# State space batches: input products ahead of the lag products, tiles shared 2, 3, 3, 3, fine rotation table by group

## The reference

```
u, q, k, v, og, glr = split(rms_norm(x) @ w_in)          # 17 column tiles of up to 128
lam_bar = exp(lam * step)                                 # complex, 32 groups x 64 states, two directions
bu = einsum('gpc,blgc->blgp', b_bar, u)                   # 16 channels a group
state_t = lam_bar * state_(t-1) + bu_t                    # forward, and reversed for the other direction
y = real(einsum('gcp,blgp->blgc', c, states)), both directions, + d * u
y = gelu(y); y = y * sigmoid(y @ w_glu)                   # the sigmoid part is in a later stage
```

## Time and profile before

| | us |
|---|---|
| median of 3 runs (2537.19 to 2540.1) | 2537.8 |
| the profiled execution, its own time | 2539.81 |
| its span | 2538.0 |
| PE busy | 2443.0 (96%) |
| DVE busy | 1531.7 (60%) |
| ACT busy | 1150.5 (45%) |
| mean granted TensorE clock | 0.986 |

### The profile page before, as it was taken

The page is one execution under the profiler, slowest core; times in us unless marked ns, Lnnn a source line. Parts: engine busy times, 40 slices in busy tenths (PEclk is TensorE's granted clock), DMA queues, the critical chain, the costliest instruction groups (busy, mean ns, idle before and its releaser), DMA issues.

```text
span 2538.0 us, 35247 instructions
## 1 busy us (share of the span) xinstructions
PE 2443.0 (96%) x14102; PEld 2075.0 (82%) x14102; DVE 1531.7 (60%) x2599; ACT 1150.5 (45%) x2010; POOL 0.2 (0%) x4
## 2 busy tenths in 40 slices
PE   7997799899999999999999999999999999999999
PEld 4887576778888999899778888778788888888887
DVE  8988756767546755564565446656886645533332
ACT  4232336344433555544454444445665443423422
POOL 0000000000000000000000000000000000000000
PEclk9998899999999999999999999999999999999999
DMA  5324532255312455444224323223334423433332
GB/s 189 95 67 103 167 111 96 80 169 191 108 59 85 156 183 184 123 132 136 78 73 157 116 81 119 75 84 101 92 92 142 132 73 88 141 99 100 92 100 91
DMA packets 109667, 289.24 MB, mean 114 GB/s; under 512 B 18913, under 2 KB 41569, under 8 KB 108225
## 3 DMA queue, kind: packets, MB, share of 16 engines
q1 hardware_dynamic: 101392, 261.36, 33.5%
q10 hardware_dynamic: 8112, 25.63, 3.1%
HBM read 265.35 MB, written 19.50 MB: 112 GB/s over the span
## 4 chain that ended last, share of the span: by engine, by line
PE 81%; DVE 12%; ACT 4%; issue 2%; DMA 1%; SPq 0%; ACTq 0%; DVEq 0%
PE ps L1414 65%; PE ps L1504 2%; PE ps L338 2%; PE ps L1479 2%; PE ps L334 2%; DVE wlo L1391 1%; PE ps L1522 1%; PE ps L1546 1%; DVE ps L1697 1%; DVE ps L1696 1%; DVE yP L1698 1%; ACT yP L1565 1%; DMA wraw<-wt 1%; DVE x L555 1%; PE ps L1446 1%
## 5 line engine op out<-in xcount | busy, mean ns | idle before, releaser
L1414 PE MATMUL ps<-in_hP,whi 128*128 128x512 f32 x1336 | 541.1, 405 | 1.6 <-issue 1.6
L1386 ACT ACTIVATE whi<-wraw 128x1024 fp32r<-128x1024 f32 x430 | 452.2, 1053 | 194.1 <-PE ps L1414 128.7
L1391 DVE TENSOR_TENSOR wlo<-wraw,whi 128x1024 fp32r<-128x1024 f32 x431 | 523.4, 1218 | 22.7 <-ACT whi L1386 22.4
L1414 PE MATMUL ps<-in_hP,wlo 128*128 128x512 f32 x1336 | 522.9, 391 | 0.0
L1414 PE MATMUL ps<-in_lP,whi 128*128 128x512 f32 x1336 | 522.1, 391 | 0.0
L1414 PE MATMUL ps<-in_hS,whi 128*128 128x256 f32 x1088 | 320.0, 294 | 5.6 <-DVE x L1719 4.3
L1414 PE MATMUL ps<-in_lS,whi 128*128 128x256 f32 x1088 | 309.4, 284 | 0.0
L1414 PE MATMUL ps<-in_hS,wlo 128*128 128x256 f32 x1088 | 309.3, 284 | 0.0
L1414 PEld LDWEIGHTS ps<-in_hP,whi 128*128 128x128 f32 x1336 | 252.4, 189 | 63.1 <-issue 11.0
L1414 PEld LDWEIGHTS ps<-in_lP,whi 128*128 128x128 f32 x1336 | 252.3, 189 | 55.5 <-issue 5.0
L1414 PEld LDWEIGHTS ps<-in_hP,wlo 128*128 128x128 f32 x1336 | 251.9, 189 | 54.2
(11 more groups left out here) (471 smaller groups left out, 3685.7 us busy)
## 6 DMA issues: line engine op xcount, KB each, us to landing
wraw<-wt SPq DMA_DIRECT2D x432, 512.0 KB, 3.5
wraw<-wt ACTq DMA_DIRECT2D x17, 512.0 KB, 4.1
k_scratch<-region_P SPq DMA_DIRECT2D x16, 256.0 KB, 3.1
v_scratch<-vtmp SPq DMA_DIRECT2D x32, 128.0 KB, 3.0
x<-x_in SPq DMA_DIRECT2D x4, 768.0 KB, 6.8
mix_u<-x SPq DMA_DIRECT2D x32, 64.0 KB, 3.4
mix_mem<-mem_in ACTq DMA_DIRECT2D x4, 512.0 KB, 6.5
x<-x_in ACTq DMA_DIRECT2D x1, 2048.0 KB, 12.7
```

Of the source, the lines that this page charges most:

```text
L1386: nc.scalar.activation(whi[:, (n + 3) % NHI, :, :], wraw[:, ws(n), :, :], ACT.Copy).then_inc(wh.sem, 1)
L1391: nc.vector.tensor_tensor(wlo[:, ws(n), :, :], wraw[:, ws(n), :, :], whi[:, (n + 3) % NHI, :, :].bitcast(F32), ALU.subtract).then_inc(wr.s ...
L1414: last = nc.tensor.matmul(ps[:, m % 2, 0:N[prod.g]], w_[:, k, :], x_[:, k, :], start=(k == 0 and j == 0), stop=(k == KT - 1 and j == 2))
```

## The change

- DVE, PE and ACT do the input side of batch b (vv, vt, bu, rot, input product) before its lag side (cl, lag, rt). The lag side and `load_mt` now come after the input product of the same batch, and before that batch's scan (cl) or behind it (rt sum).
- `dve_main` is split in three: `dve_input`, `dve_scan`, `dve_states`. pe_bu(b) for b > 0 waits for the copies of vT (vt_ready) and no longer for rt_ready.
- Tiles: 6, 7 in batch 0; then 8 to 10, 11 to 13, 14 to 16.
- Batches 1 to 3 begin with vv(b), and gelu and gelu_end of batch b-1 now come between the first two lows and rot(b).
- In the last batch high_tail(0) on ACT stands behind rt(3), and low_tail(0) on DVE behind low(16), after cl(3).
- The table fine is laid out [group, 17] instead of [17, group], and its powers are built in that layout.

```diff
-            fine = sb("s5fine", [P, 2, 17, G], on=fs)
+            fine = sb("s5fine", [P, 2, G, 17], on=fs)
 def pe_bu(pe, b):
                 pe.wait_ge(ul.sem, 16 * SC * (b + 1))
-                pe.wait_ge(rt_ready.sem, b + 1)
+                if b == 0:
+                    pe.wait_ge(rt_ready.sem, 1)
+                else:
+                    pe.wait_ge(vt_ready.sem, 2 * b + 2)
 def dve_rot(v, b):
-                f = [fine[:, i, 0:16, gs].rearrange("p c g -> p g c").unsqueeze(2).to_broadcast([P, GB, 6, 16]) for i in range(2)]
+                f = [fine[:, i, gs, 0:16].unsqueeze(2).to_broadcast([P, GB, 6, 16]) for i in range(2)]
-            BATCH = [(6, 7, 8, 9), (10, 11, 12, 17), (13, 14, 15, 17), (16, 17, 17, 17)]
+            TILES = [(6, 7), (8, 9, 10), (11, 12, 13), (14, 15, 16)]
 SP
+                    park(sp, 6)
+                    park(sp, 7)
+                    for b in range(1, NB):
+                        sp.wait_ge(y_done.sem, b)
+                        load_u(sp, b)
+                        if b > 1:
+                            park(sp, TILES[b - 1][2])
+                        store_y(sp, b - 1)
+                        t1, t2, t3 = TILES[b]
+                        park(sp, t1)
+                        load_mt(sp, b)
+                        park(sp, t2)
+                    park(sp, NT - 1)
+                    store_y(sp, NB - 1)
 PE (tile(n): the tile, then the turn of the v tile before it)
+                    pe_bu(pe, 0)
+                    tile(6)
+                    tile(7)
+                    pe_y(pe, 0)
+                    for b in range(1, NB):
+                        t1, t2, t3 = TILES[b]
+                        pe_vt(pe, b)
+                        pe_bu(pe, b)
+                        tile(t1)
+                        tile(t2)
+                        pe_lag(pe, b)
+                        tile(t3)
+                        pe_y(pe, b)
...
 ACT
+                    tile(6)
+                    tile(7)
+                    act_y(a, 0)
+                    for b in range(1, NB):
+                        t1, t2, t3 = TILES[b]
+                        act_vt(a, b)
+                        act_dec(a, b)
+                        act_tanh(a, b - 1)
+                        tile(t1)
+                        tile(t2)
+                        act_rt(a, b)
                         if b == NB - 1:
                             high_tail(a, 0)
+                        tile(t3)
                         if b == NB - 1:
                             high_tail(a, 1)
                             for k in range(6):
                                 act_mem(a, k)
                         act_y(a, b)
+                    act_mem(a, 6)
+                    act_mem(a, 7)
+                    act_tanh(a, NB - 1)
...
 DVE, tables
-                    for n in (1, 2, 4, 8):
-                        powers(fine, n, n, n, late)
+                    for n in (1, 2, 4, 8):
+                        by = [fine[:, i, :, n:n + 1].to_broadcast([P, G, n]) for i in range(2)]
+                        cmul(fine[:, 0, :, n + 1:2 * n + 1], fine[:, 1, :, n + 1:2 * n + 1], fine[:, 0, :, 1:n + 1], fine[:, 1, :, 1:n + 1],
+                             by[0], by[1], [q[:, :, 0:n] for q in grouped])
...
 DVE, batches
+                    low(v, 6)
+                    dve_input(v, 0)
+                    low(v, 7)
+                    dve_scan(v, 0)
+                    dve_states(v, 0)
+                    for b in range(1, NB):
+                        t1, t2, t3_ = TILES[b]
+                        dve_vv(v, b)
+                        low(v, t1)
+                        dve_gelu(v, b - 1)
+                        low(v, t2)
+                        dve_gelu_end(v, b - 1)
+                        dve_rot(v, b)
+                        dve_input(v, b)
+                        dve_cl(v, b)
+                        low(v, t3_)
                         if b == NB - 1:
+                            low_tail(v, 0)
+                        dve_scan(v, b)
+                        dve_rt(v, b)
+                        dve_states(v, b)
...
+                    dve_gelu(v, NB - 1)
+                    dve_gelu_end(v, NB - 1)
```

More of the change, by code:

```diff
@@ L541, in dve_rt, with dve_input @@
                     .then_inc(rt_ready.sem, 1)
[L543 to L546, removed]
+            def dve_input(v, b):
                 v.wait_ge(bu_done.sem, b + 1)
@@ L551, in dve_main, with dve_scan @@
                 cmul(g3(z_[0]), g3(z_[1]), bur, bui, er, ei, [g3(t_) for t_ in tmpA], conj=True)
-                low(v, second)
+            def dve_scan(v, b):
+                er, ei = rot[0][:, :, :], rot[1][:, :, :]
                 v.wait_ge(dec_ready.sem, b + 1)
@@ L667, in _ @@
                     pe_tile(pe, 5)
-                    before = 5
-                    for b in range(NB):
-                        t1, t2, t3, t4 = BATCH[b]
-                        pe_bu(pe, b)
[L672 to L676, removed]
-                        pe_y(pe, b)
[L678 to L697, removed]
@@ new lines, in _, with tile @@
+                    before = [5]
+                    def tile(n):
+                        pe_tile(pe, n)
+                        pe_turn_v(pe, before[0])
+                        before[0] = n
+                    pe_bu(pe, 0)
[5 more added lines that the diff above has]
+                        pe_vt(pe, b)
+                        pe_bu(pe, b)
+                        tile(t1)
+                        tile(t2)
+                        pe_lag(pe, b)
+                        tile(t3)
+                        pe_y(pe, b)
@@ new lines, in _ @@
+                    pe.wait_ge(wr_tail.sem, 1)
+                    pe.wait_ge(tf.sem, 2 * NT)
+                    for k in range(KT):
+                        pe.wait_ge(mar.sem, k + 1)
+                        for j, (w_, x_) in enumerate(((whi[:, 3], in_hP), (whi[:, 3], in_lP), (wlo[:, NT % NRAW], in_hP))):
+                            last = nc.tensor.matmul(ps[:, 0, :], w_[:, k, :], x_[:, k, :],
+                                                    start=(k == 0 and j == 0), stop=(k == KT - 1 and j == 2))
@@ L699, in _ @@
+                    last.then_inc(td_tail.sem, 1)
                 @block.scalar
@@ L738, in _, with tile @@
                     act_tile(a, 5)
-                    before = 5
-                    for b in range(NB):
-                        t1, t2, t3, t4 = BATCH[b]
+                    before = [5]
+                    def tile(n):
+                        act_tile(a, n)
+                        act_v(a, before[0])
+                        before[0] = n
+                    tile(6)
[9 more added lines that the diff above has]
+                        act_rt(a, b)
                         if b == NB - 1:
                             high_tail(a, 0)
[L744 to L748, removed]
+                        tile(t3)
                         if b == NB - 1:
@@ L753, in _ @@
                         act_y(a, b)
[L754 to L772, removed]
+                    act_mem(a, 6)
+                    act_mem(a, 7)
+                    act_tanh(a, NB - 1)
+                    nc.scalar.preload_act_table_set("natural_log_exp_and_others")
                     act_chain.close()
@@ L903, in _ @@
+                    for k in range(4):
+                        dve_mem_apply(v, k)
+                    for k in range(4):
+                        dve_mem_residue(v, k)
+                        dve_mem_apply(v, k + 4)
+                    dve_mem_residue(v, 4)
+                    dve_mem_residue(v, 5)
+                    dve_gelu(v, NB - 1)
+                    dve_gelu_end(v, NB - 1)
+                    dve_mem_residue(v, 6)
+                    dve_mem_residue(v, 7)
                     dve_chain.close()
```

48 lines of the change are left out of this document (8 added, 40 removed).

## The result

The median went from 2538.3 us (6 runs, 2535.18 to 2540.1) to 2548.69 us (6 runs, 2547.98 to 2549.45). The ratio is 1.0043, with an interval of 1.0032 to 1.0054: the kernel is slower by 10.9 us, 8.1 to 13.7 (the two medians differ by 10.4). The forecast was 2545.8, or 8.0 more than before.

The account below looks back on a forecast made before the run. Bound: one chain across engines at 94.5 to 288.6 us, VectorE nearly the bound. I3 came 13.2 us earlier, but the last batch ended at 291.3 against 283.3: +8.0, median 2545.8; range 2541 to 2551, 8 in 10 2536 to 2556.

Parts of the forecast that it names:

- The layout: Fine table by group: dve_rot priced like the input product, 5.45 us, saving 2.27 each time; hidden in batch 0.
- Batch 0 to 1: Start of input product 0 to that of 1: tanh ends at 129.7, new DVE stall of 6.0 us, I1 at 136.0.
- The cycle: One input product's start to the next, batches 1 to 3: 52.5 us each, against 51.9 before.
- mt: Transfer now directly ahead of y: loaded 8.2 us after the rt sum, bounds 7.0 to 9.5; PE stands some 4 us.
- y: PE's y up to ACT's copy: 7.2 us in batches 1 and 2, 8.3 in batch 3.
- B: Rival, short handshakes: PE at 2.4 GHz through y(1) and y(2) (5.6), tables land in 2.5 us; 2539.3 us, chance 0.20.
- D: Rival: PE's waits put all three y at 1.2 GHz, up to 11 us each; 2556 us, chance 0.12.
- The last batch: From input product 3 to the last gelu_end: ends at 291.3 against 283.27, so the rest moves by +8.0 us.
- stall of low_tail: Last batch: DVE waits 5.4 us for ACT's high_tail(0), now behind act_rt(3); the scan queues behind it.
- The memory's products: Last batch: start at 276.2, end by 288.1 and stay covered, with their loads landing in time.
- C: Rival, faster: DVE's own work bounds if transfer plus y take under 12.0 us, steps to tanh under 3.5; 2532.2, chance 0.12.
- E: Rival: rotation products stay at 1.41 us because of the coarse operand, the layout does nothing; 2552.4 us, chance 0.08.

Follow-up runs that it names:

- order_only: The changed kernel with the fine table in its old layout, keeping the new order and tile shares: 2555.83 us, ratio 1.0074 to the kernel before.
- tail_early: The changed kernel with ACT's high_tail(0) moved from behind the lag copies to behind tanh(2): 2545.21 us, ratio 1.0031 to the kernel before.
- mt_two: The changed kernel with the eight mt transfers issued half by SP, half by ACT: 2552.01 us, ratio 1.0052 to the kernel before.
- rt_early: The changed kernel with the rt sum between the scan and its four rotations in batches 1 to 3: 2545.75 us, ratio 1.0029 to the kernel before.

## Why the prediction was right, point by point

**The layout.** dve_rot takes 128.40 to 133.85 = 5.45 us, as forecast, its products 0.95 each (0.87 start to start). In batch 0 it is covered: the wait for the input product went from 2.64 to 4.87, where 2.64 + 2.27 was forecast, and the powers cost nothing that can be seen. order_only prices the rest. The Trainium skill (SBUF — State Buffer, the note on cachelines) says that SBUF reads need at least two hits to a 16-byte line for full bandwidth. Both rows of before agree: with 32 words between neighbours a product takes 1.51 us, and cl's operand with the same step, but each word 16 times, takes 0.82 for 640 columns.

**Batch 0 to 1.** The stall is there, for the tanh, with 4.29 us and not 6.0. Mis-sized was the time from vv to the tanh: I let the chain end 1.14 earlier than before, at 129.7, and gelu_end started at 127.52. Before, PE had stood 3.20 us ahead of the transposes of vv, which then took 3.68 us at a granted clock of 0.50, and ACT waited 0.68 between its two copies. After, it stood only 2.05 us, since vv came one low (1.14) sooner after I0, and the same 16 took 1.97 us at 1.00. PE in the kernel before, then after:

```profile
121.80 3.68 PE L358 MATMUL ps<-par,vv 128*128 128x128 f32 x16 [3.20 <-DVE vv L265]
```

```profile
120.15 1.97 PE L358 MATMUL ps<-par,vv 128*128 128x128 f32 x16 [2.05 <-DVE vv L265]
```

**The cycle.** The first came out to half a us, term by term in the table. The second is 1.9 longer, in two terms: mt (9.1 for 8.2) and y (8.4 for 7.2). The bounds for mt were 7.0 to 9.5. y(2) waited 4.78 us and took the price of y(3) before, which had waited 9.01; y(1) waited 1.74 and took the price of y(2) before, which had waited 1.70. My 7.2 for a wait of 4 was the wrong neighbour. The third price, of y(0), was read a little low as well: 112.92 to 118.64 is 5.72, not 5.6, which only rivals B and D use.

**The last batch.** The stall of low_tail is 5.45 us against 5.4. mt took 9.78 against 8.2, the largest miss: I had sized it alone, and it ran beside the four memory loads. SP's issue grew from 5.11 to 6.44 us, and in 270 to 281 us the DMA engines were full at 307 GB/s, as this line of the kernel after shows:

```profile
270.00:281.00 11.00, 0.38 (x2) 0.38 (x2) 6.41 (x17) 2.32 (x3) 0.00 (x0) 0.62 1.03 307
```

The memory's products, which I called covered, were so by a hair: DVE waited 4.55 us for the store of tile 15, queued behind mt on SP, a queue step that I had not followed. gelu(3) came only 0.65 us after y's copy. tail_early shows that it is the next bound.

**The sum.** -1.7 for the first stretch, -0.5 and +1.9 for the cycles, +1.8 for the last, -0.5 for the earlier start: +1.0 on the forecast +8.0, which is the 9.0 of the spans. So the forecast is nearer than its terms are: errors of 2.7 us downwards and 3.7 upwards partly cancelled, and that was luck. The medians lie a little wider apart, with 9 inside their interval.

**The rivals.** B (mt in 2.5 us, y at full clock) is out by the last landings of 3.1 to 4.5 us and the y's of 7.3 to 8.4. C's conditions failed both: R to y's copy is 15.2 us, not under 12.0, and from there to gelu_end it is 6.6, where under 3.5 was asked for the steps to the tanh. D has the right sign for y(2), at 8.4, far from 11. E is out by the products of 0.95. The Trainium skill's figure for the fixed cost (DMA: Bandwidth & Descriptors), about 2 us, would have given 2541; the trace has it otherwise, with last landings of 3.1 to 4.5 us, and mt_two shows that a second queue does not bring y earlier.

## What to carry to other kernels

Before a step is moved, name the wait that it covers where it stands: cl was 9.7 us of work over a chain of ACT and PE that DVE had to wait for, and moving it from there cost about what the new layout gained (7.9 each). A saving on an engine is worth its size only where nothing else ends last; the same layout was worth 2 us in one order and 8 in the other. Where a transfer comes onto the chain, list every other transfer of those microseconds, and what is queued behind it, before it is priced.

## What the runs showed of the hardware

- Eight transfers of 64 KB inside SBUF, in packets of 512 bytes and all out of the same 16 partitions, move at 70 to 83 GB/s whether one queue issues them or two. With two an issue takes 0.96 to 1.07 us and not 0.64. The Trainium skill (DMA: Bandwidth & Descriptors, Issuing engines are not separate DMA queues) says that issuing from several engines saves only the time of initiating. The trace agrees that the transfer gains nothing, and here not even that time was saved in full: 4.3 us for four each against 5.11 for eight on one.
- The transposes above are 1.97 us after 2.05 us of idle PE and 3.68 after 3.20. So 1.14 us of earlier work had them done 2.85 earlier after I0, two and a half times as much. The same lag products took 3.68 us after waits of up to 1.8 us (and 1.76 in rt_early), 5.35 after 2.70 in order_only, and 5.6 to 5.9 after 5.3 to 5.4, at mean granted clocks of 0.61 to 0.64. PE's waits made the step behind them longer too, and rt_early lost its gain in batch 1 to that.
